# One VectorE instruction in another place: the gate of a prompt pair ahead of a key page's turn, in slot 0 of each attention period

## The reference, cut to what matters

```
s = q @ k.T * scale + cum_q - cum_k          # per head, masked
p = softmax(s)
o = p @ v
x = x + (o * sigmoid(gate)) @ w_o
```

## Time and profile before

| | us |
|---|---|
| median of 3 runs | 2024.12 |
| the three runs | 2014.05, 2024.12, 2030.99 |
| the profiled execution, its own time | 2018.67 |
| its span in the trace | 2016.5 |

### The profile page before, as it was taken

How to read it: one execution, slowest core, us unless ns; L and a number is a source line. 1 busy time by engine, 2 the same in 40 slices (tenths; PEclk the granted TensorE clock), 3 DMA queues, 4 the chain that set the end, 5 groups by cost and what they waited for, 6 DMA issues and landing times.

```text
span 2016.5 us, 35645 instructions
## 1 busy us (share of the span) xinstructions
PE 1935.1 (96%) x14855; PEld 1779.8 (88%) x14855; DVE 1040.9 (52%) x1170; ACT 691.8 (34%) x898; POOL 440.3 (22%) x106
## 2 busy tenths in 40 slices
PE   6999999999899999999999999799998999999998
PEld 6979969979789999999999999655555999999998
DVE  4445245245446865455532535567664566646461
ACT  4131232232224325152531432244444332515251
POOL 2302402412303312121133233000001332121212
PEclk9999999999999999999999999899998999999999
DMA  5351441441243223222232221789996222222231
GB/s 162 126 165 45 137 164 46 137 157 52 95 167 95 84 68 101 82 85 83 98 94 64 65 84 44 215 233 279 280 277 222 85 84 78 90 84 96 71 104 47
DMA packets 197349, 239.13 MB, mean 119 GB/s; under 512 B 16419, under 2 KB 168355, under 8 KB 197027
## 3 DMA queue, kind: packets, MB, share of 16 engines
q1 hardware_dynamic: 175650, 183.27, 30.1%
q10 hardware_dynamic: 21488, 53.46, 8.1%
q0 software_dynamic: 80, 0.52, 0.1%
HBM read 210.77 MB, written 26.12 MB: 117 GB/s over the span
## 4 chain that ended last, share of the span: by engine, by line
PE 68%; issue 16%; DVE 6%; POOL 4%; ACT 2%; DMA 2%; SPq 1%; ACTq 1%; DVEq 0%; POOLq 0%
PE PS L800 12%; PE PS L801 11%; PE PS L802 11%; POOL w_lo L740 4%; PE PS L816 4%; PE PS L818 4%; PE PS L817 4%; PE PS L879 3%; PE PS L880 3%; PE PS L881 3%; PE PS L1349 2%; PE PS L1304 1%; PE PS L1250 1%; PE PS L1284 1%; DVE k_page_t L2366 1%
## 5 line engine op out<-in xcount | busy, mean ns | idle before, releaser
L740 POOL TENSOR_TENSOR w_lo<-w_raw,w_hi 128x2048 fp32r<-128x2048 f32 (+2 forms) x101 | 439.1, 4348 | 1543.5 <-ACT w_hi L1453 1543.5
L1453 ACT ACTIVATE w_hi<-w_raw 128x2048 fp32r<-128x2048 f32 (+2 forms) x101 | 178.1, 1764 | 644.4 <-PE PS L802 419.1
L800 PE MATMUL PS<-hidden_hi,w_hi 128*128 128x296 f32 (+1 forms) x1024 | 304.4, 297 | 0.7 <-DVE hidden_tmp L2135 0.6
L802 PE MATMUL PS<-hidden_hi,w_lo 128*128 128x296 f32 (+1 forms) x1024 | 304.7, 298 | 0.0
L801 PE MATMUL PS<-hidden_lo,w_hi 128*128 128x296 f32 (+1 forms) x1024 | 304.2, 297 | 0.0
L800 PE MATMUL PS<-x_hi,w_hi 128*128 128x296 f32 (+1 forms) x896 | 269.4, 301 | 5.4 <-DVE x_lo L1898 2.8
L801 PE MATMUL PS<-x_lo,w_hi 128*128 128x296 f32 (+1 forms) x896 | 268.4, 300 | 0.0
L802 PE MATMUL PS<-x_hi,w_lo 128*128 128x296 f32 (+1 forms) x896 | 267.8, 299 | 0.0
L879 PE MATMUL PS<-w_hi,x_hi 128*128 128x256 f32 x800 | 225.8, 282 | 0.4 <-DVE fox_gate L2287 0.4
L881 PE MATMUL PS<-w_lo,x_hi 128*128 128x256 f32 x800 | 224.8, 281 | 0.0
L880 PE MATMUL PS<-w_hi,x_lo 128*128 128x256 f32 x800 | 224.6, 281 | 0.0
(11 more groups left out here) (294 smaller groups left out, 3869.4 us busy)
## 6 DMA issues: line engine op xcount, KB each, us to landing
w_raw<-in_w_mlp_up SPq DMA_DIRECT2D x32, 1024.0 KB, 5.4
w_raw<-in_w_mlp_down SPq DMA_DIRECT2D x32, 1024.0 KB, 5.1
k_page<-in_cache_k SPq DMA_DIRECT2D x256, 128.0 KB, 5.7
v_page<-in_cache_v ACTq DMA_DIRECT2D x56, 512.0 KB, 8.0
w_raw<-in_w_ret_in SPq DMA_DIRECT2D x24, 1024.0 KB, 5.4
sample_state<-in_state_ret SPq DMA_DIRECT2D x32, 512.0 KB, 5.3
out_state_ret_sample<-sample_state ACTq DMA_DIRECT2D x32, 512.0 KB, 4.3
w_raw<-in_w_ret_out SPq DMA_DIRECT2D x16, 512.0 KB, 3.5
```

The lines of the kernel that those rows point to most:

```text
L740: pool.tensor_tensor(lo, raw, hi.bitcast(F32), ALU.subtract).then_inc(lo_done, 1)
L800: pe.matmul(o, wh[:, w], xh[:, t, cols], start=(t == 0), stop=False)
L802: last = pe.matmul(o, wl[:, w], xh[:, t, cols], start=False, stop=(t == kt - 1))
L1453: act.activation(part(WH[n.slot], n, kt), part(WR[n.slot], n, kt), ACT.Copy).then_inc(hi_done, 1)
```

## The change

In slot 0 of periods 1 to 7 VectorE's gate multiplication of the pair before comes ahead of the turn of the slot's second key page (8b + 1) instead of behind it. Slots 1, 2 and 3 keep their order, and so does period 8, which turns no page.

```diff
                     if i == 1 and v:
                         probs_copy_s(b - 1)
+                    if i == 0 and live(j - 1):
+                        gated(j - 1)
                     if k:
                         turn_page(NPAGE * b + 2 * i + 1)
-                    if i != 1 and live(j - 1):
+                    if i > 1 and live(j - 1):
                         gated(j - 1)
                     if i == 3 and v:
                         output_s(b - 1)
```

## The result

The changed kernel is slower: median 2034.00 us of 19 runs (2023.11 to 2042.48) against 2019.26 of 19 runs of before (2013.69 to 2030.99). The ratio is 1.0064, 95% interval 1.0049 to 1.0078, about 13 us. The profiled execution took 2030.31 us for a span of 2028.3, 11.8 us more than the span of before.

What follows compares the result with a forecast made beforehand. TensorE was taken as the bound. 1.15 us (period 1) + 6 x 0.35 - 0.21 - 0.09 = 2.95, say 3.0 gained: 2015.7 us by the profiled execution, 2021.1 against the median; range 2010 to 2031.

Steps and rivals of the forecast that it cites:

- the releaser that the trace of before named: Line 1271 as releaser of ScalarE's copy; disbelieved. Rival if true: copy moves too, 7.5 us gained, 2011.2, chance 0.08.
- The new wait: TensorE at line 1254 waits for ScalarE's copy of line 1804 in periods 2 to 7: 0.70 us each.
- The 0.35 us per period: Gain left in each of periods 2 to 7 from 1.05 us, after 0.70 turns into a wait at line 1254.
- The 0.21 and 0.09 us taken off for late pages: Gain lost in periods 3 and 5, where page 8b+3 comes late and the turn's slack is 0.14 and 0.26 us.
- Period 8 of before: Already had the changed order: line 1254 went 0.54 us after the copy's start, taken over for periods 2 to 7.
- The clock moves: Rival on period 6's half-clock stretch: it vanishes, 2012.5, chance 0.08; or one more comes, 2018.9, chance 0.04.
- VectorE's wait for page 8b+5: VectorE's wait before turning that page grows from 0.39 to 0.99 us, covered by 2.5 us, costing nothing.
- The slower rival: The turn of page 8b+5 passes its cover in all seven periods: 4.7 us lost, 2023.4, chance 0.07.
- The rival that the pages set the pace: Loop periods keep 29.76 us and only period 1 gains, 1.15 us: 2017.5, chance 0.18.
- the reading by the first half of what the Trainium skill says: Solid DMA engines mean DMA-bound: the loop would be bound by its pages, periods 2 to 7 gaining nothing.

Runs made afterwards that it cites:

- experiment 4: experiment 1 plus an unused VectorE maximum over 570 constants ahead of the moved gate in periods 2 to 7: 2018.58 us, ratio to before 0.9983.
- experiment 5: The changed kernel plus two tiny waited-for ScalarE instructions ahead of the slot 1 copies in periods 2 to 7: 2036.74 us, ratio to before 1.0084.
- experiment 6: The changed kernel plus 384 bias columns computed once too often ahead of line 1254 in periods 2 to 7: 2020.90 us, ratio to before 1.0003.
- experiment 8: experiment 1 with half of the bias moved between the scores' last narrow matmuls and the values product: 2011.21 us, ratio to before 0.9955.
- experiment 2: The kernel before with only ScalarE's last two value-page issues moved behind its slot 1 copies: 2021.16 us, ratio to before 1.0011.
- experiment 1: The changed kernel with ScalarE issuing a sample's last two value pages behind its slot 1 copies: 2014.83 us, ratio to before 0.9970.

## Why the prediction was wrong

**What held.** The gate started at once behind the maximum, and line 1271's idle went. The copy of line 1804 did not move, in spite of the releaser that the trace of before named; its releaser after the change is "issue". The new wait is 0.67 to 0.72 us (forecast 0.70), period 2 is 29.42 us (29.41) and period 1 lost 1.13 (1.15). The 0.35 us per period is thus right where the clock held, in periods 2 and 4. The 0.21 and 0.09 us taken off for late pages in periods 3 and 5 can't be read here, since both hold a fall; VectorE waited for no page in them. Period 8 of before, which already had the new order, was a good witness for the wait.

**The step that failed** is the rival *The clock moves*. It says "With less idle it may stay at 2.4 GHz", gives that side twice the chance, and prices the other with "one more such stretch comes: 0.2 us lost". It counted idle and not where it lies. The edit took 0.35 us of idle away and moved the rest 1.7 us down TensorE's queue, in front of the run of lines 1254, 1260, 1279 and 1284; then the clock fell in four periods, not in none or two, and at 3.2 to 4.8 us a fall, where I had one price of 3.2. In the profiled executions that is 17.5 us lost for 3.2 in before, 14 us more, against a gain of 3; by the mean clocks of all runs it is some 18. That the idle's place would bring falls in most periods stood in no case. Experiments 4 and 5 show that the place is the cause, and experiment 6 that filling the place takes the cost away. Why a run of matmuls just behind an idle matters so much is not shown: that they are small is the guess, and experiment 8, which broke them up, left it open. Period 8 of before had a fall in it too: 2.8 us behind the start of its line 1254, which had waited 0.67 us, the clock falls for 10.2 us. It would have been a hint and no proof, since in experiment 2 period 8 has no idle at line 1254 and the clock falls there 3.6 us behind that line's start. The window of before:

```profile
1537.60:1547.80 10.20, 7.39 (x46) 4.83 (x46) 1.33 (x4) 6.30 (x12) 0.00 (x0) 0.50 0.34 134
```

**A small miss.** VectorE's wait for page 8b+5 grew from 0.39 to 0.54 us in period 2, not to 0.99, because the page landed sooner (10.3 us behind its last issue, for 10.7). It cost nothing, as forecast. The slower rival, by that page, did not happen: TensorE has no wait above 0.3 us at its page scores in periods 2 to 7 of the changed kernel. The rival that the pages set the pace was wrong in its size, and so was the reading by the first half of what the Trainium skill says (Perfetto Trace Analysis, What "DMA-bound" means): experiment 1 ran a period of 28.63 us at a DMA share of 1.08. But it had a true core, which shows once the clock holds (experiment 8).

**The range** stopped at 2031 because every case in it was a matter of single stretches; it should have held a case in which each period meets one (six times 3.2 us, 19 us). Its base was high as well: the median of three, 2024.12, lies 4.9 us over the 2019.26 of 19 runs, which by luck brought the forecast of 2021.1 nearer to 2034 than its difference deserves: 3 us less than before was forecast, and 14.7 more was measured.

## What to carry to other kernels

When an edit turns one wait of TensorE into a shorter one elsewhere, look at what stands beside each of the two places, and not only at the sum: here 0.7 us of idle just in front of the narrow matmuls of line 1254 and those behind them brought the clock down in most periods, where 0.7 to 1.06 us in front of line 1271, with the wide matmuls of lines 1246 and 1250 next, did so in 2 of 24. That the next matmuls' width is the reason is not shown. Take the last wait away in the same edit, or put large matmuls that are due anyway into the gap. And if "busy" of TensorE grows with the same number of matmuls, read the granted clock by period before any chain of waits.

## What the runs showed of the hardware

In the profiled execution of the changed kernel the fall of period 5 came 1.6 us behind the start of line 1254, that of period 3 2.2 us, and in the kernel before the only fall in periods 2 to 7 came 3.3 us behind it (1476.1 for 1472.8; period 8's has been shown): in both kernels behind the same run of matmuls. (Experiments 6 and 8 have one fall each behind a wait for a page.) The windows of these falls, of the changed kernel and of before:

```profile
1385.60:1392.40 6.80, 6.80 (x25) 3.29 (x25) 3.40 (x8) 3.70 (x8) 0.00 (x0) 0.50 1.08 293
```

```profile
1472.80:1476.10 3.30, 3.24 (x25) 2.31 (x24) 2.02 (x5) 0.21 (x3) 0.00 (x0) 1.00 1.10 261
1476.10:1482.90 6.80, 6.80 (x34) 3.52 (x32) 3.25 (x5) 3.57 (x8) 0.00 (x0) 0.50 1.08 291
```

In the four falls of the changed kernel's periods 3, 5, 6 and 7 the clock stayed at 1.2 GHz for 6.8 or 10.2 us although TensorE was never idle in that time (6.80 of 6.80 us busy, and 10.20 of 10.20). The Trainium skill (TensorE: Matmul & The Clock Gate, A second HAM failure mode: psum-queue depth-cycling) tells of a kernel that loses by frequent short idles between groups of matmuls and the clock's swings that follow; the changed kernel, with idles of 0.4 and 0.7 us in a period and four falls, agrees. But the kernel before has as many idles in a period, 0.4 and 1.05 us, and one fall, so their number alone does not tell the two apart. Unexpected was how little separates the two sides: in one profiled execution each (the first of them the fastest of its kernel), 0.70 us of idle at line 1271 gave no fall in periods 2 to 7, and 0.69 us at line 1254 gave four.
